# Two-phase feed-forward of the second layer, with seven block products in place of eight and weight sums made by VectorE

## The reference

```python
def conv_ffn(h, w_up, conv_w, conv_b, w_down):        # D_MODEL 1024, D_FF 2816, CONV_W 3
    u = h @ w_up                                      # 1024 x 1024 @ 1024 x 5632
    up = jnp.pad(u, ((0, 0), (1, 1), (0, 0)))
    u = sum(up[:, j:j + T] * conv_w[j] for j in range(3)) + conv_b     # over tokens
    gate, val = jnp.split(u, 2, axis=-1)
    return (jax.nn.silu(gate) * val) @ w_down         # 1024 x 2816 @ 2816 x 1024
...
    f = conv_ffn(modulate(x, mod[3], mod[4]), w_up[l], conv_w[l], conv_b[l], w_down[l])
    x = layer_norm(DEEPNORM_ALPHA * x + mod[5] * f, ln2_g[l], ln2_b[l])
```

## Time and profile before

| | us |
|---|---|
| median of 3 runs | 3620.06 (3619.49 to 3621.11) |
| span of the profiled execution | 3623.1 |
| PE busy | 3438.2 (95%) |
| DVE busy | 1690.8 (47%) |
| ACT busy | 1040.3 (29%) |
| POOL busy | 1077.2 (30%) |
| chain that ended last: PE, DVE, issue | 84%, 9%, 3% |

### The profile page before, as it was taken

The page is one execution under the profiler, slowest core; times in us unless marked ns, Lnnn a source line. Parts: engine busy times, 40 slices in busy tenths (PEclk is TensorE's granted clock), DMA queues, the critical chain, the costliest instruction groups (busy, mean ns, idle before and its releaser), DMA issues.

```text
span 3623.1 us, 57600 instructions
## 1 busy us (share of the span) xinstructions
PE 3438.2 (95%) x24727; PEld 2833.2 (78%) x24727; DVE 1690.8 (47%) x2711; ACT 1040.3 (29%) x1485; POOL 1077.2 (30%) x412
## 2 busy tenths in 40 slices
PE   6999999988999999999999899999979989999998
PEld 5777778877778888888887677788867678888887
DVE  4333563066276343343436732463086764434436
ACT  4333564124232111111113323474143321111111
POOL 1221101302343333333333212201313344444443
PEclk9999999989999999999999899999989999999999
DMA  5111001252211111111111111001152111111111
GB/s 192 33 23 30 1 2 59 88 188 59 60 30 41 35 39 38 35 41 36 36 41 70 23 26 39 11 2 30 47 177 79 50 47 47 47 47 51 49 47 64
DMA packets 269680, 186.44 MB, mean 51 GB/s; under 512 B 45404, under 2 KB 249076, under 8 KB 269428
## 3 DMA queue, kind: packets, MB, share of 16 engines
q1 hardware_dynamic: 268272, 182.28, 16.8%
q10 hardware_dynamic: 1156, 0.48, 0.0%
HBM read 174.33 MB, written 8.39 MB: 50 GB/s over the span
## 4 chain that ended last, share of the span: by engine, by line
PE 84%; DVE 9%; issue 3%; ACT 1%; DMA 1%; POOL 1%; SPq 1%; POOLq 0%; DVEq 0%; ACTq 0%
PE psum L1146 61%; PE psum L937 6%; PE psum L1252 5%; PE psum L1410 3%; PE psum L946 2%; PE psum L1338 2%; DVE f_t L2490 1%; PE psum L1174 1%; DMA ada_late<-in_w_ada_dram 1%; DVE y_chan L2376 1%; PE psum L1369 1%; PE psum L1072 1%; DVE c_x L2340 1%; DVE h_lo L2116 1%; PE psum L1494 1%
## 5 line engine op out<-in xcount | busy, mean ns | idle before, releaser
L1146 PE MATMUL psum<-h_hi,w_split 128*128 128x512 f32 (+1 forms) x6016 | 1458.4, 370 | 15.8 <-DVEq L696 6.2
L887 POOL TENSOR_SCALAR w_split<-w_raw 128x1024 fp32r<-128x1024 f32 x196 | 550.3, 2808 | 2371.2 <-PE psum L1146 1640.8
L1146 PEld LDWEIGHTS psum<-h_hi,w_split 128*128 128x128 f32 x6016 | 1038.3, 188 | 229.4 <-issue 20.6
L1146 PE MATMUL psum<-h_lo,w_split 128*128 128x512 f32 (+1 forms) x3008 | 806.8, 368 | 0.0
L1146 PEld LDWEIGHTS psum<-h_lo,w_split 128*128 128x128 f32 x3008 | 520.0, 188 | 98.0
L2490 DVE SCALAR_TENSOR_TENSOR f_t<-psum,vec,f_t 128x1023 f32<-128x1023 f32 (+1 forms) x264 | 260.1, 1013 | 664.9 <-ACT f_t L3086 661.8
L889 POOL TENSOR_TENSOR w_split<-w_raw,w_split 128x1024 fp32r<-128x1024 f32 x196 | 480.5, 2451 | 16.4
L1146 PE MATMUL psum<-f_hi,w_split 128*128 128x512 f32 (+1 forms) x1696 | 416.9, 371 | 13.5 <-DVE f_t L2490 9.2
L3086 ACT ACTIVATE f_t<-psum,vec 128x1280 f32<-128x1280 f32 (+1 forms) x88 | 115.5, 1312 | 905.2 <-PE psum L1146 886.7
L1146 PEld LDWEIGHTS psum<-f_hi,w_split 128*128 128x128 f32 x1696 | 296.7, 188 | 77.4 <-issue 22.0
L2376 DVE SCALAR_TENSOR_TENSOR y_chan<-psum,mods,y_chan 128x1024 f32<-128x1024 f32 (+1 forms) x256 | 247.0, 1001 | 162.3 <-PE psum L1146 162.1
(11 more groups left out here) (300 smaller groups left out, 3564.9 us busy)
## 6 DMA issues: line engine op xcount, KB each, us to landing
w_raw<-in_w_up_dram SPq DMA_DIRECT2D x88, 512.0 KB, 3.8
ada_late<-in_w_ada_dram SPq DMA_DIRECT2D x32, 1024.0 KB, 7.4
w_raw<-in_w_down_dram SPq DMA_DIRECT2D x44, 512.0 KB, 3.8
w_raw<-in_w_in_dram SPq DMA_DIRECT2D x42, 512.0 KB, 3.8
ada<-in_w_ada_dram SPq DMA_DIRECT2D x4, 2048.0 KB, 16.8
ada_early<-in_w_ada_dram SPq DMA_DIRECT2D x8, 1024.0 KB, 5.3
x_first<-in_x_dram SPq DMA_DIRECT2D x8, 512.0 KB, 7.8
o_x<-in_x_dram SPq DMA_DIRECT2D x8, 512.0 KB, 3.9
```

The lines of the kernel that those rows point to most:

```text
L887: pool.tensor_scalar(w_hi[:, n % 2], w_raw[:, n % 2], 1.0, None, ALU.mult).then_inc(s["w_hi_done"], 1)
L1146: last = pe.matmul(columns(key, t0, t0 + tn), weight, a[:, k, t0:t0 + tn], start=(k == order[0] and j == 0), stop=(closes and k == order[- ...
```

## The change

The feed-forward of the last layer becomes two phases.

Up phase. The feature tiles 0 to 5 are computed as before. For the tiles 6 to 21 (16 of them) the product of a tile, 1024 channels by 256 columns (gate and value) times 1024 tokens, is read as a 2 by 2 product of blocks: channels in two halves of 512, columns gate or value, tokens in two halves of 512. It is made by seven block products in place of eight (`fast_up`), each of 12 matmuls of 128x512: 84 for a feature tile, where there were 96. Four operands on the weight side are sums or differences of blocks, made for each feature tile by DVE (`weight_sums`, four instructions of 128x512). Those on the token side are made once: `differences(k)` for k = 0 to 3, 13 DVE and 3 ACT instructions of 128x512 each, placed among the tiles 4 and 5, and `last_differences`, which overwrites a part of `h_hi` and `h_lo` when the last ordinary product has ended. Each weight operand is split by one ACT instruction (`high_operand`) and one of POOL (`low`), both 128x512. Partial results are taken out of PSUM by ACT (`take`, four of 128x512) and joined by DVE (`joined`, three of 128x512) into `up_u` in SBUF; `begin` and `conv` then read `up_u`, not PSUM. The gated tiles are no longer split and multiplied at once: SP stores each in DRAM (`f_mid`).

Down phase (`down_by_token`). All 22 feature tiles are multiplied by token tile, first the tokens 0 to 511, then 512 to 1023: 44 steps of 24 matmuls of 128x512 into 8 banks of PSUM. For every step the 128 rows of `w_down` (512 KB) and the half of the gated tile (256 KB) are loaded, five buffers deep; DVE multiplies the weights by the sub-layer's gate and makes the low part of the tokens, ACT makes both high parts, POOL the low part of the weights. DVE no longer adds Y to `y_chan`; `y_chan` is stored in DRAM and read back (4 MB) for the transposes. The last two steps of each half run token tile by token tile; the four tiles of the first half are normalised and stored during the second, the other four at the end.

Cut to its core:

```diff
+FAST_FROM = {DEPTH - 1: 6}
+LAST_STEPS = 2
@@ PE
+            def fast_up(l):
+                def product(i, j, bank, x_hi, x_lo, begins=True):
+                    n = 7 * i + j
+                    hi, lo = up_ops[n % 4][:, 0], up_ops[n % 4][:, 1]
+                    wait((s["op_ready"], n + 1))
+                    for k in range(KT // 2):
+                        for pass_, (w, a) in enumerate(((hi, x_hi), (hi, x_lo), (lo, x_hi))):
+                            last = pe.matmul(psum[:, bank, :], w[:, P * k:P * k + P], a[:, k], ...)
+                    last.then_inc(s["prod_done"], 1)
+                for i in range(N_FAST):
+                    if i >= 2:
+                        wait((s["snap_done"], 4 * (i - 2) + 4))
+                    product(i, 0, x_bank(i), *tokens(low, 0))
+                    if i:
+                        wait((s["u_done"], 3 * (i - 1) + 3))
+                    else:
+                        wait(freed("F", l, fast_f - 1, 0))
+                        wait((s["t_ready"], 16))
+                    product(i, 1, Z_BANK, *tokens(low, 1))
+                    wait((s["snap_done"], 4 * i + 1))
+                    product(i, 2, x_bank(i), t2_hi, t2_lo, begins=False)
+                    wait((s["u_done"], 3 * (i - 1) + 1) if i else None)
+                    product(i, 3, Y_BANK, *tokens(high, 0))
+                    wait((s["snap_done"], 4 * i + 3))
+                    product(i, 4, x_bank(i), t3_hi, t3_lo, begins=False)
+                    product(i, 5, Z_BANK, *tokens(high, 1), begins=False)
+                    wait((s["u_done"], 3 * i + 2))
+                    product(i, 6, x_bank(i), t4_hi, t4_lo, begins=False)
@@ DVE, one feature tile
+                        if i:
+                            conv(f - 1, 1)
+                            gated(f - 1)
+                        if i == N_FAST - 1:
+                            gate_weights(0)
+                        weight_sums(i, True)
+                        if i + 1 < N_FAST:
+                            weight_sums(i + 1, False)
+                        for n in range(3):
+                            dve.wait_ge(s["snap_done"], 4 * i + (1, 2, 3)[n])
+                            joined(i, n)
+                        conv(f, 0)
@@ ACT, one feature tile
+                        ahead(0)
+                        if i:
+                            take(i - 1, 3)
+                            begin(f - 1, 1)
+                        take(i, 0)
+                        ahead(1)
+                        take(i, 1)
+                        ahead(2)
+                        take(i, 2)
+                        ahead(3)
+                        ahead(4)
+                        ahead(5)
+                        if i == N_FAST - 1:
+                            high_weights(0)
+                        begin(f, 0)
+                        ahead(6)
+                        silu(f)
@@ DVE, down phase
+                for n in range(2, 2 * FT):
+                    if n == FT + 3:
+                        for i in range(3):
+                            last_norm(i)
+                    if n == FT + 4:
+                        last_norm(3)
+                    gate_weights(n)
+                    low_tokens(n)
+                for i in range(4, NTL):
+                    last_norm(i)
```

More of the change, by code:

```diff
@@ L239, in __init__ @@
                 self.gemm(("out", l, m), ("W", l, m))
+            if l in FAST_FROM:
+                for f in range(FAST_FROM[l]):
+                    for half in range(2):
+                        self.gemm(("up", l, f, half), ("F", l, f, half))
+                continue
             for i in range(NPAIR + 1):
@@ L1686, in phase_f @@
                     moments_at[7] = partial(spread_gates, l)
+                if l in FAST_FROM:
+                    for f in range(2, fast_f):
+                        for half in range(2):
+                            gemm(("up", l, f, half), ("F", l, f, half), groups(l), between=moments_at if (f, half) == (2, 0) else {})
+                    fast_up(l)
+                    return down_by_token(l)
                 for i in range(NPAIR + 1):
@@ L2481, in conv @@
                     key = ("F", l, f, half)
-                    w = f_t[:, half]
-                    acc = slot(*key)
+                    fast = l in FAST_FROM and f >= fast_f
+                    w = f_t[:, 1] if half else gate_of(l, f)
+                    acc = up_u[:, half] if fast else slot(*key)
                     dve.wait_ge(s["conv_start"], nth("conv", l, f, half))
@@ new lines, in two_phases @@
+                def two_phases():
+                    gated(0)
+                    for half in range(2):
+                        conv(1, half)
+                    gated(1)
+                    conv(2, 0)
+                    for k in range(3):
+                        residual(k)
+                    conv(2, 1)
+                    gated(2)
+                    for k in range(3, 6):
+                        residual(k)
+                    conv(3, 0)
+                    for k in range(6, 8):
+                        residual(k)
+                    conv(3, 1)
+                    gated(3)
+                    dve.wait_ge(s["r_stored"], 2 * 16 * KT)
+                    differences(0)
+                    conv(4, 0)
+                    differences(1)
+                    conv(4, 1)
+                    gated(4)
+                    differences(2)
+                    conv(5, 0)
+                    differences(3)
+                    weight_sums(0, False)
+                    last_differences()
+                    conv(5, 1)
+                    gated(5)
+                    for i in range(N_FAST):
+                        f = fast_f + i
+                        if i:
+                            conv(f - 1, 1)
[9 more added lines that the diff above has]
+                        conv(f, 0)
+                    low_tokens(0)
+                    low_tokens(1)
+                    gate_weights(1)
+                    conv(FT - 1, 1)
+                    gated(FT - 1)
+                    return s["a_whole"], nth("ff", l, FT - 1)
@@ L3098, in high_half, with high_differences, last_high_differences @@
                     say("a_hi_ready", copy(f_hi[:, f // 2 % 2, f % 2, 0:w], f_t[:, 0, 0:w]))
+                def high_differences(k):
+                    for n, (whole, t_hi) in enumerate(((taken[:, 1], t3_hi), (taken[:, 0], t2_hi), (taken[:, 2], t4_hi))):
+                        act.wait_ge(s["t_whole"], 3 * k + n + 1)
+                        say("t_split_hi", copy(t_hi[:, k], whole))
+                def last_high_differences():
+                    act.wait_ge(*full("F", l, fast_f - 1, 1))
+                    for k in range(4):
+                        say("t_split_hi", copy(h_hi[:, k, HALF:LAT], t_one[:, k]))
```

510 lines of the change are left out of this document (421 added, 89 removed).

## The result

| | before | after |
|---|---|---|
| median, us | 3619.77 (3618.74 to 3621.11, 4 runs) | 3641.83 (3640.38 to 3646.95, 4 runs) |
| ratio | | 1.0066, 95% interval 1.0052 to 1.0081 |
| span of the profiled execution | 3623.1 | 3641.0 |
| PE busy; matmuls | 3438.2; 24727 | 3417.9; 24535 |
| DVE, ACT, POOL busy | 1690.8, 1040.3, 1077.2 | 1797.6, 1193.2, 1063.6 |

Slower by 22 us, where 192 matmuls fewer had been expected to bring nothing (+2) and the edges with their clock to cost 28. The two profiled executions differ by 6.5 us already ahead of the change, in code that both share. A row that both traces have shows it: the copy of the spread gates, made while TensorE computes tile 2 (the tile gate_row: duration min/median/max, first and last start; before, then after).

What follows compares the result with a forecast made beforehand. PE was taken as the only bound before the change, and a ring through the engines' lists after it. Terms of 2 + 24 + 17 + 6 + 1.4 - 20.2 gave +30, so 3650 us against the median, range 3612 to 3678.

Steps and rivals of the forecast that it cites:

- the edges with their clock: Entry, down phase, tail and slower clock behind their waits, less the 20.2 us lost before: expected to cost 28.
- the sum +30: All terms over the stretch and its tail: 2 + 24 + 17 + 6 + 1.4 - 20.2 us.
- The ring: Sixteen seven-product tiles: strict engine lists form a chain of 21.9 us a tile against 21.76, +2 us in all.
- Entry: Before the first block products: DVE is late, product 0 starts about 97 us in, PE waits 21 and 3: +24 us.
- third step: Down phase: operands of step 3 come late behind 5.5 MB of loads, +3 us, between 0 and 10.
- Clock: Entry and start of the down phase: PE runs slower behind long waits, 3 us lost each, +6 us.
- Waiting for POOL: Up tiles: one POOL difference falls on the gate half's taps, about 0.9 us a tile.
- the taps do not wait: Rival for the up tiles: taps never wait for POOL, 3636 us, still slower; chance 0.17.
- PE keeps the pace: Rival for the up tiles: the chain closes within 19.04 us, tiles bring their 43.5, 3604 us; chance 0.13.
- Down phase: PE sets the steps' pace; waits of 6 at the start, 3 at step 3, 8 at the half: +17 us.
- the clock falls in the ring: Rival for the up tiles: a tile in two loses 3 us, 3675 us; chance 0.12, together with other waits.
- Tail: After the last matmul: DVE ends 8.5 us behind it, against 7.0 before, +1.4 us.

Runs made afterwards that it cites:

- act_order: Changed kernel with ACT's fourth taking and begin of the value half moved ahead of the silu: 3604.1 us.
- sums_first: Changed kernel with DVE's third and fourth weight sums moved ahead of the value half's taps and gated product: ratio 1.0017 to before.
- small_low: Changed kernel with POOL making the low halves of the weight operands over 32 of 512 columns, part of the computation left out: ratio 1.0021 to before.
- best_7: best_8 with seven products from tile 7 on, differences at tiles 4, 5 (twice) and 6: 3572.2 us.
- short_diffs: Changed kernel with token differences made of the high halves alone, 24 half-size DVE instructions fewer ahead of product 0: 3627.4 us.
- from_8: Changed kernel with seven products only from tile 8 on, differences at tiles 6 and 7: 3639.5 us.
- spread_8: from_8 with the four groups of differences spread over tiles 4, 5 and 6 (twice): 3632.9 us.
- best_14: best_8 with seven products only from tile 14 on and the differences at tiles 10 to 12: 3584.7 us.
- best_8: Changed kernel combining act_order, sums_first, spread_8, down_start, three last steps sum by sum, third step's weights gated before the last taps: 3580.7 us.
- down_start: Changed kernel with the first two down steps' tokens split before the last tile's begin and taps, stored sums read later: ratio 1.0062 to before.

## Why the prediction came out as it did

The forecast of 3650 was 8 us above 3641.8; the sum +30 stands against +24.4 from the gates. The mechanism on which it rested is the one that was found; ring, entry and third step were put too high and the clock too low, and part of the closeness is that these offset each other, which is luck.

- **The ring**, the step on which it rested: 21.9 predicted, 21.64 measured, with waits before products 2 and 4 for ACT's takings. act_order shows that it was the cause. The prediction followed one chain, the one that ends before product 4; sums_first shows a second of nearly the same length, which ends before product 2. The term was +2; the steady tiles gave 16 x (21.64 - 21.76) = -2.
- **Waiting for POOL**: 0.9 a tile predicted, 0.92 read (3.52 - 2.60), 0.9 by small_low. That two weight sums wait 1.0 us each as well was not in the sum, and costs the ring 0.1 at most. Taps of `up_u` do wait, which those of the earlier trace rows never did; "the taps do not wait" falls. The joinings, with one input in PSUM, never waited (691 to 693 ns). The Trainium skill ("SBUF — State Buffer", Who interferes with whom) says both: two inputs in SBUF contend with GpSimd's reads, one does not. These rows agree.
- **"PE keeps the pace"** failed as a forecast, but by 2.6 us of order and not for want of engine time: act_order is at 19.4 and 3604 us, where the prediction had put this rival; best_7 is at 19.1.
- **Entry**: 97 us to product 0 predicted, 97.8 measured, 21.6 lost. The other 3 of the +24 were for product 1, which waited 0.98. Right in size, and short_diffs bears out DVE as the path. What the term did not see is that the place of the work counts beside its sum: I had added up DVE's work from tile 2 on; from_8, spread_8 and best_14 show the place.
- **Down phase**: start 6 predicted, 6.0; half 8, 7.7; the third step 3, none. So 13.7 for 17. The wait at the half came in two parts (4.74 and 2.97), not in three, and a part of it by another way: the third norm waited 2.36 us until the first one's store had left the buffer that they share, and SP had issued that store behind two loads.
- **Clock** +6: product 0 ran at 0.62 over 6.1 us (2 lost), the first steps at 0.72 over 9.8 (3), the half at 0.54, 9.4 us of work (4): 9. The sum had none for the half. Between the short pauses in the tiles the clock stayed at 1.00, so "the clock falls in the ring" falls.
- **Tail** 8.5 predicted; DVE ends at 3637.7, the last matmul at 3629.1: 8.6.

The account: entry 21.6, sixteen tiles 3006.0 to 3354.2 = 348.2 against 16 x 21.76, 0; waits of the down phase 13.7, its clock 7; tail 8.6 - 7.0 = 1.6; less the 20.2 of before: +23.7 for the 24.4 measured. Predicted for entry, ring and their clock 24 + 2 + 3 = 29, for the down phase 17 + 3; measured 21.6 and 20.7: mis-sized by 7 too much and 1 too little.

## What to carry to other kernels

Before work is taken off the bounding engine, lay out one round of the pipeline as a ring through every engine's written list: engines that are 40 to 60% busy can set the pace between them, and a saving then buys nothing until an instruction is moved (here two instructions of ACT past a silu were worth 37 us, where the matmuls left out are 43.5). One-off work packed into a few tiles reappears as a wait, and the long ones here were followed by a lower clock; spreading it helped only in part as long as one piece, with what follows it, was longer than a product. That shorter pieces cure it is a guess that no run tests. Waits at a phase's edge come in layers; expect the next one before promising the time.

## What the runs showed of the hardware

- A pause of PE costs more than its idle row: in a steady tile 0.95 + 0.60 us stand as waits, 2.6 are lost. From the starts of the matmuls at 3078.83 to 3100.45, beyond the pitch of 0.2267: 1.12 and 0.75 before products 2 and 4, that is the wait and the 0.16 by which a row of 0.39 overlaps the next one in a full stream; 0.14 and 0.11 within the twelve matmuls behind each (rows of 3.02 and 2.99 us, where one without a pause is 2.88). The other 0.46 stand before and in product 6, which starts at 3091.01 behind the second joining (ends at 3090.96) and has no row of a wait.
- Pauses of 0.6 to 1.7 us, two a tile, left the granted clock at 1.00 (its upper level) over 348 us. Behind waits of 4.2 us and more it was lower: 0.86 over the 10 us behind 4.2, 0.69 over 10 behind 4.7 (best_8), 0.73 over 10 behind 5.2 (spread_8), 0.72 over 10 behind 6.0, 0.62 over 6 behind 11.1, 0.54 over 13 at the half, around 4.7 and 3.0. Waits between 2.6 and 3.3 us went either way: 1.00 over 3.9 us behind 2.98 (down_start) and over 20 around 3.10 (short_diffs), but 0.53 over 3.5 us behind 2.67 (spread_8) and 0.67 over 4.5 behind 3.26 (down_start).
- The start of the stretch under study moved by up to 12 us between executions, in code that no edit touched (the gates' copy at 2900.8 to 2912.8), as much as some of the effects sought. A row that all traces share removes it.
